# Mixer heads: the stabiliser rows broadcast by one product on a rounded part and a remainder; the convolution's spreads on four row quarters at a time

## The reference, cut to what matters

```python
def mlstm_chunkwise(q, k, v, ig, lf):
    ...
        b = jnp.cumsum(lfc, axis=-1)
        logw = b[..., :, None] - b[..., None, :] + igc[..., None, :]
        logw = jnp.where(causal, logw, -jnp.inf)
        g = b + m[..., None]
        m_t = jnp.maximum(g, jnp.max(logw, axis=-1))
        w = jnp.exp(logw - m_t[..., None])
        ...
        s = jnp.einsum("bhtd,bhsd->bhts", qc, kc) * w
...
def mixer(...):
    ...
    a = glu_a * jax.nn.sigmoid(glu_b)
    a = causal_depthwise_conv(a, w_dw, b_dw)
    a = jax.nn.silu(group_layer_norm(a, N_CONV_GROUPS, g_cn, b_cn))
    return jnp.concatenate([h_m, a], axis=-1) @ w_out.astype(h.dtype)
```

## Time and profile before

| | us |
|---|---|
| time, median of 3 runs (2279.96 to 2281.94) | 2281.36 |
| span of the profiled execution, first to last instruction | 2274.4 |
| the difference, outside the span | 6.96 |
| PE busy in the span | 2222.0 |
| DVE busy | 1280.8 |
| POOL busy | 1131.6 |
| ACT busy | 992.0 |

### The profile page before, as it was taken

How to read it: one execution, slowest core, us unless ns; L and a number is a source line. 1 busy time by engine, 2 the same in 40 slices (tenths; PEclk the granted TensorE clock), 3 DMA queues, 4 the chain that set the end, 5 groups by cost and what they waited for, 6 DMA issues and landing times.

```text
span 2274.4 us, 28727 instructions
## 1 busy us (share of the span) xinstructions
PE 2222.0 (98%) x10450; PEld 1749.5 (77%) x10450; DVE 1280.8 (56%) x2061; ACT 992.0 (44%) x1630; POOL 1131.6 (50%) x596
## 2 busy tenths in 40 slices
PE   8999999999999999999999999999999999999998
PEld 5886667788888878766778888887767688888886
DVE  4999847863546699984365122157776653221222
ACT  4368543333232335875344223244666653331323
POOL 2698833554444639876374344463422244444442
PEclk9999999999999999999999999999999999999999
DMA  8432205354646323221122323232222122333332
GB/s 319 138 98 71 65 29 172 120 185 157 231 166 217 96 77 94 75 84 38 56 84 86 99 93 101 87 108 72 82 57 65 47 92 94 103 92 97 97 99 86
DMA packets 206662, 240.39 MB, mean 106 GB/s; under 512 B 9762, under 2 KB 172378, under 8 KB 206554
## 3 DMA queue, kind: packets, MB, share of 16 engines
q1 hardware_dynamic: 205990, 238.76, 32.9%
q10 hardware_dynamic: 564, 0.21, 0.0%
HBM read 236.84 MB, written 2.10 MB: 105 GB/s over the span
## 4 chain that ended last, share of the span: by engine, by line
PE 52%; DVE 3%; POOL 2%; issue 2%; ACT 1%; DMA 0%; DVEq 0%; POOLq 0%; ACTq 0%; SPq 0%
PE product L2508 16%; PE product L2510 15%; PE product L2509 15%; DVE side L1888 1%; PE side L3076 1%; POOL ring_low L950 1%; PE product L3111 1%; POOL slot_f L981 1%; PE side L3096 1%; POOL slot_f L1003 1%; PE product L2881 1%; PE side L2865 0%; PE side L3023 0%; DVE slot_f L1888 0%; ACT sqt L1436 0%
## 5 line engine op out<-in xcount | busy, mean ns | idle before, releaser
L950 POOL TENSOR_TENSOR ring_low<-ring_f,ring_high 128x1024 fp32r<-128x1024 f32 (+1 forms) x349 | 845.6, 2427 | 1029.2 <-ACT ring_high L1076 1028.8
L2508 PE MATMUL product<-slot_r,ring_high 128*128 128x512 f32 (+1 forms) x2536 | 1007.1, 397 | 13.5 <-ACT slot_f L1282 4.0
L2510 PE MATMUL product<-slot_r,ring_high 128*128 128x512 f32 (+1 forms) x2536 | 989.3, 390 | 0.0
L2509 PE MATMUL product<-slot_r,ring_low 128*128 128x512 f32 (+1 forms) x2536 | 988.3, 390 | 0.0
L1076 ACT ACTIVATE ring_high<-ring_f 128x1024 fp32r<-128x1024 f32 (+1 forms) x349 | 367.8, 1056 | 697.9 <-DMA ring_f<-in_w_ff 326.0
L2508 PEld LDWEIGHTS product<-slot_r,ring_high 128*128 128x128 f32 (+1 forms) x2536 | 475.9, 188 | 146.4 <-issue 35.5
L2510 PEld LDWEIGHTS product<-slot_r,ring_high 128*128 128x128 f32 (+1 forms) x2536 | 475.9, 188 | 101.5
L2509 PEld LDWEIGHTS product<-slot_r,ring_low 128*128 128x128 f32 (+1 forms) x2536 | 476.4, 188 | 97.0 <-issue 1.4
L1845 DVE SCALAR_TENSOR_TENSOR va<-product,sqt 128x512 f32<-128x512 f32 x96 | 66.3, 692 | 332.9 <-ACT sqt L1154 331.6
L1888 DVE SCALAR_TENSOR_TENSOR side<-slot_f,cols,side 128x512 f32<-128x512 f32 x322 | 214.8, 747 | 0.0
L1865 DVE TENSOR_TENSOR slot_f<-product,slot_f 128x512 f32<-128x512 f32 x64 | 44.2, 691 | 161.6 <-PE product L2510 161.6
(11 more groups left out here) (325 smaller groups left out, 2164.8 us busy)
## 6 DMA issues: line engine op xcount, KB each, us to landing
ring_f<-in_w_ff SPq DMA_DIRECT2D x128, 512.0 KB, 3.8
slot_f<-in_w_ada SPq DMA_DIRECT2D x48, 1024.0 KB, 7.4
ring_f<-in_w_in SPq DMA_DIRECT2D x96, 512.0 KB, 3.9
ring_f<-in_w_out SPq DMA_DIRECT2D x40, 512.0 KB, 3.4
ring_f<-in_w_up SPq DMA_DIRECT2D x32, 512.0 KB, 3.7
ring_f<-in_w_down SPq DMA_DIRECT2D x32, 512.0 KB, 3.6
slot_f<-in_x SPq DMA_DIRECT2D x4, 512.0 KB, 5.0
ring_f<-in_w_v SPq DMA_DIRECT2D x4, 512.0 KB, 3.5
```

The lines of the kernel that those rows point to most:

```text
L950: pool.tensor_tensor(whole(ring_low[:, s, :, :], n), whole(ring_f[:, s, :, :], n), whole(ring_high[:, s, :, :], n).bitcast(F32), ALU.subtr ...
L2508: pe.matmul(out_ap, high, rhs_high, start=start, stop=False)
L2509: pe.matmul(out_ap, low, rhs_high, start=False, stop=False)
L2510: return pe.matmul(out_ap, high, rhs_low, start=False, stop=stop)
```

## The change

Before, the stabiliser's product is made on float32 rows. Now ACT copies `max_row` into the first four rows of a new tile `max_parts` in the rounded type, DVE writes the remainder (float32 row less rounded row) to rows 32 to 35, and the rest of the 36 rows is zero. The product takes all 36 rows by a column of `neg_pick`, which is -1 at row hd and at row 32 + hd, in the rounded type. ACT's copy stands before its sigmoid of tile 2 of z, DVE's subtraction before the centring of convolution tiles 6 and 7, and DVE fills `neg_pick` and the zeros once at the kernel's start. The new waits are folded into two existing signals, which now count 2.

The spreads are now made for four tiles at once, one on each row quarter, in two calls: tiles 0 to 3 after `weighted_values(0, 2)`, and tiles 4 to 7 after `denominator(0)`.

```diff
+        PART_ROWS = 32 + HEADS
+        max_parts = sb("max_parts", [PART_ROWS, T], F32R)
+        neg_pick = sb("neg_pick", [PART_ROWS, HEADS], F32R)
...
-        neg_ident = small[0:HEADS, 60:64]
...
                     if t == 2:
                         wait(act, place, acol_done, 1)
                         act.activation(a_cols, PM[1][:, 0:BLK * HEADS], ACT.Copy).then_inc(acol_ready.sem, 1)
+                        wait(act, place, mrow_ready, BLK)
+                        act.activation(max_parts[0:HEADS, :], max_row, ACT.Copy).then_inc(acol_ready.sem, 1)
                     act.activation(tile(SE, t), bank(o)[:], ACT.Sigmoid).then_inc(taken[o % 4].sem, 1)
...
-            steps.did(dve.tensor_scalar(neg_ident, ident[0:HEADS, 0:HEADS], -1.0, None, ALU.mult))
+            steps.did(dve.scalar_tensor_tensor(neg_pick[:], ident[0:PART_ROWS, 0:HEADS], -1.0,
+                                               ident[0:PART_ROWS, 32:32 + HEADS], ALU.mult, ALU.subtract))
+            steps.did(dve.tensor_scalar(max_parts[:], ones[0:PART_ROWS, 0:1].to_broadcast([PART_ROWS, T]), 0.0, None,
+                                        ALU.mult))
...
                     centre_conv(4, 5)
+                wait(dve, place, acol_ready, 2)
+                dve.tensor_tensor(max_parts[32:PART_ROWS, :], max_row, max_parts[0:HEADS, :].bitcast(F32),
+                                  ALU.subtract).then_inc(gate_steps.sem, 1)
                 centre_conv(6, 7)
...
                         wait(pe, place, cxc_ready, NT - 1)
-                    pe.matmul(PM[0][:], neg_ident[:, hd:hd + 1].to_broadcast([HEADS, P]), max_row,
+                        wait(pe, place, gate_steps, 2)
+                    pe.matmul(PM[0][:], neg_pick[:, hd:hd + 1].to_broadcast([PART_ROWS, P]), max_parts[:],
                               start=True, stop=True).then_inc(bc_done.sem, 1)
...
-                def conv_spreads(t0):
-                    for t in (t0, t0 + 1):
-                        if t < 2:
-                            wait(pe, place, crn_small, 1)
+                def conv_spreads(half):
+                    tiles = range(BLK * half, BLK * half + BLK)
+                    if half == 0:
+                        wait(pe, place, crn_small, 1)
+                        wait(pe, place, p_ready, BLK)
+                        for t in (0, 1):
                             wait_bank(pe, place, o_outa(t))
-                        elif t < 4:
-                            wait(pe, place, p_ready, BLK)
-                        else:
-                            wait(pe, place, cy_ready, t - 3)
+                    else:
+                        wait(pe, place, cy_ready, BLK)
                     for s in range(BLK):
-                        for t in (t0, t0 + 1):
-                            ins = quarter_spread(spread_bank(t)[:, s * P:(s + 1) * P], t % 4, t // 4 * BLK + s)
+                        for t in tiles:
+                            ins = quarter_spread(spread_bank(t)[:, s * P:(s + 1) * P], t % 4, half * BLK + s)
...
                 scores(0, 3)
+                weighted_values(0, 2)
                 conv_spreads(0)
-                weighted_values(0, 2)
-                conv_spreads(2)
                 stabiliser(1)
-                conv_spreads(4)
                 weighted_values(0, 3)
-                conv_spreads(6)
                 denominator(0)
+                conv_spreads(1)
                 conv_product(0)
```

More of the change, by code:

```diff
@@ L530, in program @@
         gates_done = Signal(sem("gates_done"), 1)
-        gates_biased = Signal(sem("gates_biased"), 1)
+        gate_steps = Signal(sem("gates_biased_then_stabilizer_split"), 2)
         fg_done = Signal(sem("forget_rows_done"), 1)
@@ L536, in program @@
         acol_done = Signal(sem("a_columns_done"), 1)
-        acol_ready = Signal(sem("a_columns_ready"), 1)
+        acol_ready = Signal(sem("a_columns_then_stabilizer_high_ready"), 2)
         em_ready = Signal(sem("denominator_floor_ready"), 1)
@@ L2054, in bias_gates @@
                     wait(dve, place, vtr_done, 8)
-                    dve.tensor_scalar(gate_parts, PM[0][:], bgate_all, None, ALU.add).then_inc(gates_biased.sem, 1)
+                    dve.tensor_scalar(gate_parts, PM[0][:], bgate_all, None, ALU.add).then_inc(gate_steps.sem, 1)
                 def gate_rows():
-                    wait(dve, place, gates_biased, 1)
+                    wait(dve, place, gate_steps, 1)
                     wait(dve, place, lsig_ready, 1)
@@ L2819, in _ @@
                 gate_product(0)
-                wait(pe, place, gates_biased, 1)
+                wait(pe, place, gate_steps, 1)
                 pe.matmul(forget_gates, gate_pick[:, HEADS:2 * HEADS], gate_parts, start=True, stop=True).then_inc(fg_done.sem, 1)
```

## The result

The changed kernel takes 2288.51 us (median of 7 executions, 2284.53 to 2292.77), the kernel before 2281.36 in the same comparison: a ratio of 1.0032, with a 95% interval of 1.0021 to 1.0042. It is slower by 0.32%, about 7 us, where no difference had been forecast. The mean granted clock of TensorE over the span, which each execution reports, is 0.988 or 0.989 in all seven. The kernel before has 0.991 to 0.994 in 28 of the 30 executions of a later comparison.

The account below looks back on a forecast made before the run. PE looked 98% busy, but the bound changes between PE, DVE's chain and POOL. Each layer +0.73 - 0.72 = +0.01, plus POOL's +0.10 and +0.60, gave 2282.1 us; range 2278.4 to 2285.5.

Parts of the forecast that it names:

- The stabiliser's product: On PE, four times a layer: 0.33 us instead of 1.05; only head 3's saving of 0.72 reaches the end.
- The spreads: On PE in head 0: a four-tile call takes 1.10 us, four quarters beside each other; PE's work falls by 2.15.
- the rival of two at a time: Spreads calls run two quarters at a time, 2.18 us instead of 1.10: 2286.4 us, slower by 0.22%; chance 0.07.
- DVE's later chain: Head 0: DVE's normed tiles release the first output product at 291.07 instead of 290.34, +0.73 us a layer.
- The subtraction: DVE's step making the stabiliser's parts, beside POOL's centring: POOL held up 0.60 us in each layer, bounds 0 and 0.69.
- the 0.60 us on POOL: Hold-up of POOL's centring by DVE's subtraction, each layer; +0.10 reaches the values in layer 0, +0.60 in layer 1.
- The step from span to median: Median of the runs taken as 6.96 us above the traced span, a part the change does not touch.
- The sum without the clock: Both layers: +0.01 us each, plus +0.10 and +0.60 for POOL, 0.72 on the median, giving 2282.1 us.
- POOL's 0.70: POOL's hold-up in the sum: +0.10 us in layer 0 and +0.60 in layer 1.
- the clock's rival: TensorE's clock falls in head 0, 1.7 us a layer: 2283.8 or 2285.5 us, still within 0.2%; chance 0.16.
- would lie between the two: Head 0's PE load placed between 1.63 of 3.60 us busy (clock stayed) and 1.17 of 3.40 (clock fell).
- none of its waits take it back: Head 1 moves by the same 0.73 us as head 0's output product, and its waits absorb none of it.

Follow-up runs that it names:

- e1: Changed kernel with the spreads put back to calls for two tiles in the old places, the new stabiliser kept: 2280.50 us.
- e3: Changed kernel with unread products in both PE gaps of head 0, one before the second spreads call, two before the first output product: 2280.59 us.
- f2: Changed kernel with two unread products only in head 0's second gap, ahead of the first output product: 2281.42 us.
- f3: Kernel with the new stabiliser and old spreads, with DVE's normed 5 put ahead of its remainder of tile 1: 2284.66 us.
- e4: Changed kernel with only the first spreads call on four tiles, the second divided into tiles 4 and 5, then 6 and 7: 2287.70 us.

## Why the prediction was wrong, step by step

- **The stabiliser's product**: 0.43 us instead of the 0.33 taken, so 0.62 saved and not 0.72. The 0.10 added to the 0.23 for a change of row groups had no row behind it; what stands there is 0.20. The places were right but one: head 1 gives it back at the values (0.88 us of wait in e1, 0.26 before) and not, as the prediction has it, at the denominator, which waits 1.73 with it and without it. Head 3's product did reach the end: in layer 0 the delay is 5.87 ahead of it (320.17 before, 326.04 after) and 5.24 behind it.
- **The spreads**: 1.11 us for a call of four tiles, against 1.10 forecast. Four quarters do run beside each other; the rival of two at a time falls.
- **DVE's later chain**: the waits were forecast as 1.3 and 2.0 us and are 1.13 and 1.96. Against the first values of head 0, from which the forecast counts, the first output product is later by 0.78 in layer 0 (1.78 - 1.00) and 0.65 in layer 1 (7.82 - 7.17), against 0.73 forecast.
- **The subtraction**: the 0.60 us on POOL, and so the 0.70 in the sum, were wrong. POOL's centring keeps its 3.62 us for four beside it, as in the earlier trace rows, and layer 1's first values wait 1.14 instead of 0.63, 0.51 more, while the stabiliser's product in front of them became shorter by 0.55. In layer 0 the first values come 0.29 sooner against what lies ahead of the stage (1.29 to 1.00 later), where 0.10 later was booked. It is DVE that pays: its two subtractions, each with a POOL instruction beside it, took 1.01 and 0.92 us instead of the 0.69 of the earlier trace rows. The Trainium skill, page "SBUF — State Buffer", section "Who interferes with whom", says that the order of issue decides which of the two is blocked. The trace agrees in layer 1, where POOL's centring starts at 1033.59 and the subtraction at 1033.69; in layer 0 both start at 272.69, so no order is shown there. A hold-up for the whole of the other, as the prediction had it, is not what these two show: beside a centring of 0.92 DVE loses 0.32 and 0.23, and POOL nothing.

The two of them in after (instructions of the line: ns min, median, max):

```profile
L2096 DVE TENSOR_TENSOR max_parts<-ada_acc,max_parts x2: 915/962/1010, 272.7 to 1033.7; 4x512 fp32r<-4x512 f32 x2
```

POOL's centring beside the first of them, in POOL's timeline:

```profile
269.99 3.62 POOL L1005 TENSOR_SCALAR slot_f<-slot_f,small 128x256 f32<-128x256 f32 x4
```

- **The step from span to median**: the 6.96 us were taken as a fixed part outside the span; it is 1.8 in every execution of after. The sum on the median does not change by that.
- **The sum without the clock** was right within what can be measured, but for POOL's 0.70: the terms as measured come to about -0.2 (-0.29 + 0.78 - 0.63 in layer 0, -0.04 + 0.65 - 0.63 in layer 1), against +0.72. No run can tell the two: e3 and f2, where the gaps are filled, have 2280.59 and 2281.42, against a forecast of 2282.1 and the 2281.3 and 2281.5 of before.
- **The failed step is the clock's rival.** It had the mechanism, and the place, and three of its numbers were wrong. The first is the work. The chance was set at 0.16 because head 0 "would lie between the two" cases of the earlier trace rows, with 1.8 us of work from 286.7 to 291.1. By the prediction's own timeline it is 1.1: of these 4.4 us, 1.3 and 2.0 are the waits that it had just worked out, and only the second call of the spreads lies between them. That is not between the two rows but emptier than the one behind which the clock fell, 1.17 of 3.40. The trace has 1.17 of 3.41 at 288.12, with the fall behind it. The second number is the chance of 0.16 that rested on this. The third is the price: one stretch a layer, 1.7 us. In layer 0 of the traced execution the stage lost 3.95 us: the first fall delays PE by 1.30 (from 1.78 to 3.08 later, at head 1's first scores, 295.93 before and 299.01 after), the delay slides DVE's remainders into POOL's work, the wait of 2.75 us that follows brings a second fall, twice as long, and only then does a saved 0.63 come back. And "none of its waits take it back" held for a shift of about 0.5 (in f2 head 1 waits 0.88 and 1.73, as in e1), not for one of 1.8. So a case that had been booked as no difference was the likely one, and slower.

The share of PE that had been read first, 98%, says nothing of this: after has 97%.

What stays open: why the same gaps bring the fall in one layer of an execution and not in the other (1.17 of 3.41 us busy at 288.12 and at 1061.20, with 0.50 and 1.00 behind them; in f3 a wait of 2.60 with the fall and one of 2.83 without), and how the 7 us of the medians divide between the two layers, since only one execution of each kernel has a trace.

## What to carry to other kernels

Where PE's work is made shorter than the chain that releases the next work, do not book the gap as a harmless wait: compare it, and the work around it, with places of the trace where the clock fell, and price what stands behind it at half speed, with the waits that the delay opens further on. The same gap will not bring the fall every time. Before shortening work on a nearly full TensorE, look for other work that can stand in the gap; here, moving one denominator behind two scores was worth more than both parts of the change. Where the times of one program spread over nearly 14 us (e4), read the granted clock of each execution before looking for a cause in the lists.

## What the runs showed of the hardware that was not expected

- Two unread products of 0.78 us each (1.56 us at 289.73 in f2) took 7 us off the changed kernel, and one in the earlier gap took nothing off.
- One program (e4) ran at 2278.04 and at 2291.77 us, with a mean clock of 0.993 and 0.987.
- An elementwise remainder on DVE took 2.85 us beside a POOL instruction of 2.53, against 0.68 alone; POOL's side was not measurably longer beside DVE's subtraction (0.92 us for each centring, as before), but its addition beside the last two remainders took 1.43 us (307.29), against 1.00 for the same one before.
